# GpSimd's order around the half-tile norms, and evacuations ahead of sums in the last group

## The chip, the cores and the metric

The kernel runs on one core of a Trainium2 chip. The metric is the device time of one execution in microseconds (us). Five engines take part, each with its own queue that runs strictly in program order: TensorE (PE in the profile), VectorE (DVE), ScalarE (ACT), GpSimd (POOL) and SyncE (SP), which starts the DMAs. They wait for each other by semaphores.

## The reference

Three transformer-like blocks follow each other on a sequence of 1024 tokens of width 1024, all in float32.

```python
def reference(x, ...):
    x = first_block(x, ...)    # rmsnorm, conformer branch + HGRN2 branch, gates, w_out, rmsnorm
    x = second_block(x, ...)   # rmsnorm, attention / short conv / spatial gating, w_out, MLP, rmsnorm
    return third_block(x, ...) # mLSTM + pooling, w_out, layernorm, MLP, layernorm
```

What matters here are the places where a product's output is normed and goes into the next product:

```python
# end of the first block, start of the second
h_res = h_res + merged @ w_out                       # OUT1
x = rmsnorm(h_res[:, N_META:], final_g)
proj = rms_norm(x, mix_norm_g) @ w_in_2              # SGU, QKV, SHORT
# the second block's MLP
x = x + mixed @ w_out_2                              # OUT2
hdn = jnp.square(relu(rms_norm(x, mlp_norm_g) @ w_up))
x = x + hdn @ w_down                                 # MLP2
x = rms_norm(x, final_norm_g)
# the third block
u = x @ w_in_3                                       # GATES3 ...
x = layer_norm_3(ALPHA * x + y @ w_out_3, ...)       # OUT3
x = layer_norm_3(ALPHA * x + squared_relu_mlp(x, w_ff1, w_ff2), ...)   # MLP3
```

## The kernel before

**Layout.** Activations are kept transposed: 8 tiles `k` of 128 channels x 1024 tokens. A weight matrix is cut into 318 slabs of 128 x 1024; a slab makes one output tile of 128 channels from all 8 input tiles (or, in the MLP's way down, two tiles from four). Slab numbers start at `OUT1` = 88, `SGU` = 100, `OUT2` = 126, `MLP2` = 138, `GATES3` = 210, `OUT3` = 235, `MLP3` = 247.

**Products.** Each float32 operand is split into a high part (rounded to the matmul's format) and a low part (the rest). A product is three matmuls per input tile and 512 tokens: `hh` x `wh`, `hh` x `wl`, `hl` x `wh` (function `three`, L489, matmul at L505). So a slab needs

- `raw`, its weights by DMA, two buffers;
- `wh`, the rounded copy, by ScalarE (`split`, L1185), which waits until PE is through with the slab two before;
- `wl` = `raw` - `wh`, by GpSimd (`split`, L3114), two halves of 128 x 512, which PE waits for one by one; and
- for the first product after a norm, `hh` and `hl` of the tiles. ScalarE makes `hh` (`half_high`, L1494; `last_high`, L1928 to L1932, with the norm's offset). VectorE makes `hl` of tiles 0, 1, 2, 4 and 6, GpSimd that of tiles 3, 5 and 7 (`GP_TILES`; `half_low`, L3136).

**Half tiles.** Before each of four norms the last four output tiles are computed twice over, first for tokens 0 to 511 (half 0), then for 512 to 1023 (half 1): `gemm_half`. While PE computes half 1, the norm of half 0 is made. The stage behind the norm begins with four slabs for half 0, then the same four for half 1 (the weights are loaded and split again). The four places are OUT1 to `SGU` (norm `nx2`), OUT2 to `MLP2` (`ff2`), the end of MLP2 to `GATES3` (`nx3`), and OUT3 to `MLP3` (`ff3`).

**The norm itself.** VectorE evacuates a tile from PSUM, adding the residual (L2334, L2572, L2658, L2954). ScalarE squares it. VectorE adds the square to a sum over the tiles (L2345, L2583, L2893; for a layernorm the values too, L2885). When the last tile is added, PE multiplies the sums by ones to get a sum per token (L769, L934, L578 and L582), ScalarE and VectorE make the root and its inverse of it, and PE spreads these over the partitions (L588). VectorE multiplies the tiles with them (L2366, L2594, L2664, L2920 to L2923), reading the rows from PSUM. PE's part of the half-1 norm is a side job: it is issued between the products of the next stage's first slabs, the token sums after the fifth to seventh tile of the first one.

**What sets the order.** Each engine's program is written out by hand. `split(n)` makes all slabs up to `n` that are not made yet, so the place of a call sets how early a slab's parts stand in a queue. In `half_lows` GpSimd makes a slab's `wl` and the tiles' `hl` in turn; ScalarE's loops `for m, tiles in ...` do the same with `wh`, the squares and `hh`.

**The last group.** MLP3 ends with half tiles too, for tiles 2 to 7: PE writes each into one of two pairs of PSUM banks in turn (12 matmuls a tile), so a tile can start only when the tile two before is evacuated (`last_sums`, L3015). VectorE also subtracts an early mean from the tiles (`less_mean_2`, L3022), adds squares (`add_square`, L2893) and the values of the last tile (`last_value`, L2899), and norms the first half (`minus`, L3030, and `times`, L3036). PE's token sums for half 0 (`rest`, L578 and L582) are issued after the sixth tile step of half 1, that is two steps into its second product.

Of the kernel before, what the change touches and what calls it, by code (L numbers as in the profile page):

```python
# [57 lines left out]
SGU, QKV, SHORT, OUT2, MLP2 = 100, 108, 120, 126, 138  # L58
# [182 lines left out]
def program(nc, A, tables, draft):  # L241
# [929 lines left out]
    def scalar():  # L1171
# [4 lines left out]
        def split(n):  # L1176

            while done[0] <= min(n, NSLAB - 1):
                i = done[0]
                done[0] += 1  # L1180
                s = i % 2
                se.wait_ge(*c.weight_in[s](i))
                if i >= 2:
                    se.wait_ge(*spent(i - 2))
                se.activation(wh[:, s, :], raw[:, s, :], COPY).then_inc(*c.hi.tick(i))  # L1185
# [310 lines left out]
        def squares_out(m, *hf):  # L1496
            se.wait_ge(*c.ev_v("out", m, *hf))
            for n, (st, scale) in enumerate((("o1", 1.0), ("o2", V("final_g", m)))):
                dst, x = out_square(m, n), X[:, m, :]
                if m > 3:  # L1500
                    se.wait_ge(*(c.acc_v(st, 4, *hf) if m == 7 else c.acc_v(st, m - 3)))
                    dst, x = side_of(dst, *hf), side_of(x, *hf)
                se.activation(dst, x, SQUARE, scale=scale).then_inc(*c.sq.tick(st, m, *hf))
# [9 lines left out]
        def out_high(k, hf):  # L1513
            half_high("nx2", k, hf, half_slot(Cb[:, 4:8, :], k), c.nrm("nx2", k, hf))
# [11 lines left out]
        squares_out(7, 0)  # L1526
        split(OUT1 + 9)
        roots_out(0)
        for m, tiles in ((5, (0, 1)), (6, (2, 3, 4)), (7, (5, 6))):
            split(OUT1 + m + 5)  # L1530
            squares_out(m - 1, 1)
            for k in tiles:
                out_high(k, 0)
        squares_out(7, 1)
        split(SGU + 1)
        out_high(7, 0)
        roots_out(1)


# [150 lines left out]
        def half_mean_root(st, hf):  # L1690
            se.wait_ge(*c.tok(st, hf))
            se.activation(rr[:, 0, 4 * hf:4 * hf + 4], aux.of("tok", st, hf)[:, 0:4], SQRT, scale=1.0 / 1024,
                          bias=EPS).then_inc(*c.root.tick(st, hf))

        def mlp_high(k, hf):
            half_high("ff2", k, hf, half_slot(xn, k), c.nrm("ff2", k, hf))
# [42 lines left out]
        square("n5", 7, c.ev_v("x2", 7, 0), 0)  # L1739
        split(OUT2 + 9)  # L1740
        half_mean_root("n5", 0)
        for m, tiles in ((5, (0, 1)), (6, (2, 3, 4)), (7, (5, 6))):
            split(OUT2 + m + 5)
            square("n5", m - 1, c.ev_v("x2", m - 1, 1), 1)
            for k in tiles:
                mlp_high(k, 0)
        square("n5", 7, c.ev_v("x2", 7, 1), 1)
        split(MLP2 + 1)
        mlp_high(7, 0)
        half_mean_root("n5", 1)  # L1750
        first_ups(MLP2, t5, hdh, mlp_high)

# [18 lines left out]
        def in_high(k, hf):  # L1771
            half_high("nx3", k, hf, side_of(X[:, k, :], hf), c.nrm("fin2", k, hf))

        mlp(MLP2, t5, hdh)
        for hf, tiles in ((0, ((), (), (), ())), (1, ((), (0, 1), (2, 3, 4), (5, 6)))):
            i = down_at(MLP2, 7, 0, hf)
            split(i + 1)
            if hf:
                half_mean_root("n6", 0)
            for j in range(4):  # L1780
                if j:
                    split(i + j + 1)
                    square("n6", 2 * j - 1, c.ev_v("dn", MLP2, 7, 2 * j - 1, hf), hf)
                for k in tiles[j]:
                    in_high(k, 0)
                square("n6", 2 * j, c.ev_v("dn", MLP2, 7, 2 * j, hf), hf)
            square("n6", 7, c.ev_v("dn", MLP2, 7, 7, hf), hf)
        split(GATES3 + 1)
        in_high(7, 0)
        half_mean_root("n6", 1)  # L1790


# [163 lines left out]
        half_square("v1", 7, 0, c.ev_v("x3", 7, 0))  # L1956
        split(OUT3 + 9)
        half_root("v1", 0)
        todo = {5: (0, 1), 6: (2, 3, 4), 7: (5, 6)}
        for m in range(5, 8):  # L1960
            split(OUT3 + m + 5)
            half_square("v1", m - 1, 1, c.ev_v("x3", m - 1, 1))
            for k in todo[m]:
                last_high(k, 0)
        half_square("v1", 7, 1, c.ev_v("x3", 7, 1))
        split(MLP3 + 1)
        last_high(7, 0)
        half_root("v1", 1)

        first_ups(MLP3, t7, hdh3, last_high)  # L1970
# [46 lines left out]
    def vector():  # L2017
# [1037 lines left out]
            less_mean_2(k, 1)  # L3055
        last_sums(6, 0)
        add_square("v2", 3, 0)
        add_square("v2", 4, 0)
        for k in (5, 6, 7):
            less_mean_2(k, 1)  # L3060
        add_square("v2", 5, 0)
        last_sums(7, 0)
        last_value(0)
        add_square("v2", 6, 0)
        add_square("v2", 7, 0)
        half_stats("v2", 0)
        less_mean_2(0, 1)
        less_mean_2(1, 1)
        last_sums(2, 1)
        minus(0, 0)  # L3070
        minus(1, 0)
        add_square("v2", 1, 1)
        last_sums(3, 1)
        times(0, 0)
        times(1, 0)
        add_square("v2", 2, 1)
# [23 lines left out]
    def gpsimd():  # L3100
# [37 lines left out]
        def half_lows(ver, first, src):  # L3138

            for hf in range(2):  # L3140
                split(first + 4 * hf + 3)
                half_low(ver, 3, hf, src(3, hf))
                half_low(ver, 5, hf, src(5, hf))
                split(first + 4 * hf + 4)
                half_low(ver, 7, hf, src(7, hf))


        split(1)
# [492 lines left out]
```

## Time and profile before

| | us |
|---|---|
| runs shown, median (lowest to highest) | 3795.52 (3794.46 to 3797.2) |
| the profiled execution | 3796.67 |
| its span | 3795.4 |
| PE busy | 3690.3 |
| VectorE busy | 1720.7 |
| ScalarE busy | 1178.2 |
| GpSimd busy | 1091.7 |

All times in the rows below are from the span's start. "Busy" of PE covers overlapping matmuls, so it is not its peak. In a timeline a row is one instruction (or, with x2 and more, a run of like ones): start, duration, engine, line, operation, what it writes and reads. In square brackets stands the idle time before it that a semaphore ended, with the engine that released it. In a row of a stretch the busy time of each engine in it has the number of its instructions behind it, in brackets; the three numbers at the end are the mean granted clock of PE as a share of full speed, the DMA engines' share, and GB/s. `B` is the large buffer with the tiles (`X` in the code), `acc` and `t` are sums and squares.

### The profile page before, as it was taken

What the parts mean: (1) busy time and instruction counts of PE and PEld (TensorE: products, weight loads), DVE (VectorE), ACT (ScalarE), POOL (GpSimd) and SP (SyncE); (2) the same over time, 40 slices, a digit from 0 to 9 for tenths busy, and PEclk for the clock granted to TensorE, in tenths of its full rate; (3) what the DMA queues carried; (4) which work ended last, traced back from release to release, by engine and by line L of the source; (5) the groups of instructions that cost most, each with busy time, mean ns of one, the idle gap of its engine ahead of it and who ended that gap; (6) DMA issues with size and microseconds to landing.
All of it is one profiled execution on the core that took longest, in us unless ns stands there. A gap on an engine that the chain in (4) does not pass through costs nothing.

```text
span 3795.4 us, 42159 instructions
## 1 busy us (share of the span) xinstructions
PE 3690.3 (97%) x17644; PEld 3015.8 (79%) x17644; DVE 1720.7 (45%) x2132; ACT 1178.2 (31%) x1523; POOL 1091.7 (29%) x747
## 2 busy tenths in 40 slices
PE   6999999999999999999999999999999999999998
PEld 6989887888878876777788888887777788888886
DVE  5665615999543472225432222225667642222226
ACT  5555423222231344443321211114322331121113
POOL 3333321222233441112432222225113342222223
PEclk9999999999999999999999999999999999999999
DMA  2011021111232341101321111113101221111112
GB/s 102 28 30 33 23 78 50 56 56 56 72 137 96 103 132 35 37 27 36 106 67 50 45 48 48 46 49 126 44 28 51 89 72 45 51 45 47 48 46 76
DMA packets 64988, 229.29 MB, mean 60 GB/s; under 512 B 7200, under 2 KB 7328, under 8 KB 64672
## 3 DMA queue, kind: packets, MB, share of 16 engines
q1 hardware_dynamic: 64800, 226.60, 18.2%
q8 instruction: 140, 2.29, 0.2%
q14 instruction: 48, 0.39, 0.0%
HBM read 201.40 MB, written 25.17 MB: 60 GB/s over the span
## 4 chain that ended last, share of the span: by engine, by line
PE 88%; DVE 7%; ACT 2%; issue 1%; POOL 1%; DMA 1%; SPq 0%; DVEq 0%; ACTq 0%
PE psum L505 77%; PE psum L853 2%; PE psum L617 2%; PE psum L868 2%; PE psum L883 1%; DVE work L2171 1%; PE psum L588 1%; PE psum L739 0%; POOL wl L3114 0%; PE psum L702 0%; DVE qb L2173 0%; PE psum L641 0%; PE psum L640 0%; DVE fb L2094 0%; DVE k L2828 0%
## 5 line engine op out<-in xcount | busy, mean ns | idle before, releaser
L3114 POOL TENSOR_TENSOR wl<-raw,wh 128x512 fp32r<-128x512 f32 x636 | 882.7, 1408 | 2378.3 <-ACT wh L1185 2378.3
L505 PE MATMUL psum<-hh,wh 128*128 128x512 f32 (+2 forms) x3760 | 1186.8, 391 | 38.4 <-POOL wl L3114 15.7
L505 PE MATMUL psum<-hh,wl 128*128 128x512 f32 (+2 forms) x3760 | 1150.2, 382 | 0.0
L505 PE MATMUL psum<-hl,wh 128*128 128x512 f32 (+2 forms) x3760 | 1145.3, 380 | 0.0
L505 PEld LDWEIGHTS psum<-hh,wh 128*128 128x128 f32 x3760 | 676.2, 190 | 185.4 <-issue 30.9
L505 PEld LDWEIGHTS psum<-hh,wl 128*128 128x128 f32 x3760 | 699.4, 190 | 134.5
L505 PEld LDWEIGHTS psum<-hl,wh 128*128 128x128 f32 x3760 | 698.5, 190 | 133.2
L1185 ACT ACTIVATE wh<-raw 128x1024 fp32r<-128x1024 f32 x318 | 335.1, 1054 | 791.5 <-PE psum L505 785.0
L505 PE MATMUL psum<-hdh,wh 128*128 128x512 f32 x1024 | 333.9, 398 | 5.0 <-DVE B L3015 4.4
L505 PE MATMUL psum<-hdh,wl 128*128 128x512 f32 x1024 | 331.1, 395 | 0.0
L505 PE MATMUL psum<-hdl,wh 128*128 128x512 f32 x1024 | 331.1, 396 | 0.0
L2652 DVE TENSOR_TENSOR B<-B,psum 128x1024 f32<-128x1024 f32 x106 | 129.5, 1222 | 419.4 <-PE psum L505 419.4
L2632 DVE TENSOR_TENSOR t<-t 128x1024 f32<-128x1024 f32 (+1 forms) x72 | 90.5, 1257 | 471.1 <-ACT t L1764 471.1
L2222 DVE SCALAR_TENSOR_TENSOR psum<-av,vec,psum 128x1024 f32<-128x1024 f32 x232 | 299.2, 1290 | 7.8
L505 PEld LDWEIGHTS psum<-hdh,wh 128*128 128x128 f32 x1024 | 191.3, 188 | 57.7 <-DVE B L3015 6.1
L505 PEld LDWEIGHTS psum<-hdl,wh 128*128 128x128 f32 x1024 | 192.4, 188 | 46.4
L505 PEld LDWEIGHTS psum<-hdh,wl 128*128 128x128 f32 x1024 | 192.4, 188 | 45.9
L1764 ACT ACTIVATE t<-psum 128x1024 f32<-128x1024 f32 x56 | 57.4, 1024 | 426.2 <-PE psum L505 426.2
L3156 POOL TENSOR_TENSOR work<-fb 128x1024 f32<-128x1024 f32 x48 | 100.6, 2103 | 188.3 <-PE psum L617 140.1
L2493 DVE CUSTOM_DVE_ANT_0 pp<-psum,bias 128x640 f32<-128x640 f32 (+2 forms) x64 | 42.1, 658 | 194.4 <-PE psum L853 106.9
L2634 DVE TENSOR_TENSOR hdl<-t,hdh 128x1024 fp32r<-128x1024 f32 (+1 forms) x72 | 83.6, 1161 | 82.7 <-ACT hdh L1767 63.0
L1767 ACT ACTIVATE hdh<-t 128x1024 fp32r<-128x1024 f32 x56 | 59.3, 1059 | 72.3 <-DVE t L2632 72.3
(422 smaller groups left out, 3019.3 us busy)
## 6 DMA issues: line engine op xcount, KB each, us to landing
raw<-in_wts SPq DMA_DIRECT2D x318, 512.0 KB, 3.5
keep_x<-B SPq DMA_DIRECT2D x14, 512.0 KB, 5.8
X<-in_xin SPq DMA_DIRECT2D x8, 520.0 KB, 5.2
keep_sz<-tmp SPq DMA_DIRECT2D x8, 512.0 KB, 2.9
av<-keep_gr SPq DMA_DIRECT2D x8, 512.0 KB, 3.4
tmp<-keep_sz SPq DMA_DIRECT2D x8, 512.0 KB, 3.5
av<-keep_gc SPq DMA_DIRECT2D x8, 512.0 KB, 3.8
xc<-keep_x SPq DMA_DIRECT2D x8, 512.0 KB, 5.8
```

Of the source, the lines that this page charges most:

```text
L505: ins = pe.matmul(out, w, x[:, k, c0:c0 + width], start=first and n == 0, stop=final and n == 2)
L617: ins = pe.matmul(x[:, n * 128:(n + 1) * 128], left[:, cc], right[:, cc], start=True, stop=True)
L853: ins = pe.matmul(sp[:, a0:a0 + wd], qa[lo:lo + 64, s, i * 128:(i + 1) * 128], ka[lo:lo + 64, s, k0 + a0:k0 + a0 + wd], start=True, stop=True)
L868: ins = pe.matmul(OUT[:, 64 * i:64 * i + 64], pt_slot(j, m)[:, b_ * 128:(b_ + 1) * 128], va[:, s, a0:a0 + 64], start=(b_ == 0), stop=(b_ = ...
L1185: se.activation(wh[:, s, :], raw[:, s, :], COPY).then_inc(*c.hi.tick(i))
L1767: se.activation(xh[:, k, :], q, COPY).then_inc(*c.ml_act.tick("hi", base, u))
L2222: ve.scalar_tensor_tensor(Cb[:, m, :] if last else taps, u[:, j:j + T], V("conv_w", 8 * j + m), taps, MUL, ADD).then_inc(*c.cv_dve.tick(*( ...
L2632: ve.tensor_tensor(q, q, q, MUL).then_inc(*c.ml_dve.tick("sq", base, u, *hf))
L2634: ve.tensor_tensor(xl, q, fp(xh), SUB).then_inc(*c.ml_dve.tick("lo", base, u, *hf))
L2652: ve.tensor_tensor(X[:, m, :], X[:, m, :], flat(pairs.of(i, e)), ADD).then_inc(*c.ev_v.tick("dn", base, g, m))
L3114: gp.tensor_tensor(wl[:, s, a], raw[:, s, a], fp(wh[:, s, a]), SUB).then_inc(*c.lo.tick(i, p))
L3156: gp.tensor_tensor(lev(lv).rearrange("p (n b) -> p n b", b=2 * hs), bv, bv[:, :, hs - 1:hs].to_broadcast([P, T // (2 * hs), 2 * hs]), SUB) ...
```

## The change

It has three parts.

1. GpSimd (`half_lows`): at each of the eight places (four norms, two halves) the `wl` of the next half's first slab stands behind the low part of tile 3, ahead of those of 5 and 7. Before, it stood behind 5.
2. ScalarE: the high part of tile 7 (half 0) moves up to those of 5 and 6, and the `wh` of the stage's second slab goes ahead of the square of tile 7 (half 1).
3. VectorE, in the last group: the evacuation of tile 7 (half 0) stands ahead of the additions of squares 4 and 5, that of tile 2 (half 1) ahead of the addition of square 7 (half 0), that of tile 3 (half 1) one place forward.

```diff
@@ -1526,14 +1526,13 @@
         squares_out(7, 0)
         split(OUT1 + 9)
         roots_out(0)
-        for m, tiles in ((5, (0, 1)), (6, (2, 3, 4)), (7, (5, 6))):
+        for m, tiles in ((5, (0, 1)), (6, (2, 3, 4)), (7, (5, 6, 7))):
             split(OUT1 + m + 5)
             squares_out(m - 1, 1)
             for k in tiles:
                 out_high(k, 0)
+        split(SGU + 1)
         squares_out(7, 1)
-        split(SGU + 1)
-        out_high(7, 0)
         roots_out(1)
...
@@ -1772,11 +1770,12 @@
             half_high("nx3", k, hf, side_of(X[:, k, :], hf), c.nrm("fin2", k, hf))
 
         mlp(MLP2, t5, hdh)
-        for hf, tiles in ((0, ((), (), (), ())), (1, ((), (0, 1), (2, 3, 4), (5, 6)))):
+        for hf, tiles in ((0, ((), (), (), ())), (1, ((), (0, 1), (2, 3, 4), (5, 6, 7)))):
             i = down_at(MLP2, 7, 0, hf)
-            split(i + 1)
             if hf:
                 half_mean_root("n6", 0)
+            else:
+                split(i + 1)
             for j in range(4):
                 if j:
                     split(i + j + 1)
@@ -1784,9 +1783,8 @@
                 for k in tiles[j]:
                     in_high(k, 0)
                 square("n6", 2 * j, c.ev_v("dn", MLP2, 7, 2 * j, hf), hf)
+            split(i + 5)
             square("n6", 7, c.ev_v("dn", MLP2, 7, 7, hf), hf)
-        split(GATES3 + 1)
-        in_high(7, 0)
         half_mean_root("n6", 1)
@@ -1956,15 +1954,14 @@
         half_square("v1", 7, 0, c.ev_v("x3", 7, 0))
         split(OUT3 + 9)
         half_root("v1", 0)
-        todo = {5: (0, 1), 6: (2, 3, 4), 7: (5, 6)}
+        todo = {5: (0, 1), 6: (2, 3, 4), 7: (5, 6, 7)}
         for m in range(5, 8):
             split(OUT3 + m + 5)
             half_square("v1", m - 1, 1, c.ev_v("x3", m - 1, 1))
             for k in todo[m]:
                 last_high(k, 0)
+        split(MLP3 + 1)
         half_square("v1", 7, 1, c.ev_v("x3", 7, 1))
-        split(MLP3 + 1)
-        last_high(7, 0)
         half_root("v1", 1)
 
         first_ups(MLP3, t7, hdh3, last_high)
@@ -3055,22 +3052,22 @@
             less_mean_2(k, 1)
         last_sums(6, 0)
         add_square("v2", 3, 0)
+        last_sums(7, 0)
         add_square("v2", 4, 0)
         for k in (5, 6, 7):
             less_mean_2(k, 1)
         add_square("v2", 5, 0)
-        last_sums(7, 0)
         last_value(0)
         add_square("v2", 6, 0)
+        last_sums(2, 1)
         add_square("v2", 7, 0)
         half_stats("v2", 0)
         less_mean_2(0, 1)
         less_mean_2(1, 1)
-        last_sums(2, 1)
+        last_sums(3, 1)
         minus(0, 0)
         minus(1, 0)
         add_square("v2", 1, 1)
-        last_sums(3, 1)
         times(0, 0)
         times(1, 0)
         add_square("v2", 2, 1)
...
@@ -3138,11 +3135,9 @@
         def half_lows(ver, first, src):
 
             for hf in range(2):
-                split(first + 4 * hf + 3)
-                half_low(ver, 3, hf, src(3, hf))
-                half_low(ver, 5, hf, src(5, hf))
-                split(first + 4 * hf + 4)
-                half_low(ver, 7, hf, src(7, hf))
+                for n, k in enumerate(GP_TILES):
+                    split(first + 4 * hf + 3 + min(n, 1))
+                    half_low(ver, k, hf, src(k, hf))
 
 
         split(1)
```

The second hunk (norm `n5`, at `MLP2`), left out, is the first one's with other names. The instructions are the same in number and kind.

GpSimd, from the end of OUT3 (the run of 20 `wl` ends with the slab before `MLP3`'s first) into MLP3, before; `hl` are low parts of tiles, 3 and 5 in the first row of two, 7 in the next row:

```order
L3114 TENSOR_TENSOR wl<-raw,wh 128x512 x20
L3136 TENSOR_TENSOR hl<-B,hh 128x512 x2
L3114 TENSOR_TENSOR wl<-raw,wh 128x512 x2
L3136 TENSOR_TENSOR hl<-B,hh 128x512
L3114 TENSOR_TENSOR wl<-raw,wh 128x512 x6
L3136 TENSOR_TENSOR hl<-B,hh 128x512 x2
L3114 TENSOR_TENSOR wl<-raw,wh 128x512 x2
L3136 TENSOR_TENSOR hl<-B,hh 128x512
L3114 TENSOR_TENSOR wl<-raw,wh 128x512 x126
```

and now:

```order
L3111 TENSOR_TENSOR wl<-raw,wh 128x512 x20
L3133 TENSOR_TENSOR hl<-B,hh 128x512
L3111 TENSOR_TENSOR wl<-raw,wh 128x512 x2
L3133 TENSOR_TENSOR hl<-B,hh 128x512 x2
L3111 TENSOR_TENSOR wl<-raw,wh 128x512 x6
L3133 TENSOR_TENSOR hl<-B,hh 128x512
L3111 TENSOR_TENSOR wl<-raw,wh 128x512 x2
L3133 TENSOR_TENSOR hl<-B,hh 128x512 x2
L3111 TENSOR_TENSOR wl<-raw,wh 128x512 x126
```

The pair of `wl` is one slab. It changed places with the low part of tile 5, in both halves.

ScalarE, at the same place, from the `wh` of the first slab of `MLP3` on, before (L1916 is a square, L1928 with L1930 a high part of tile 5 or 7, L1932 that of another tile):

```order
L1185 ACTIVATE wh<-raw 128x1024
L1916 ACTIVATE t<-B 128x512
L1928 ACTIVATE B<-B,vec 128x512
L1930 ACTIVATE hh<-B 128x512
L1932 ACTIVATE hh<-B,vec 128x512
L1916 ACTIVATE t<-B 128x512
L1185 ACTIVATE wh<-raw 128x1024
L1928 ACTIVATE B<-B,vec 128x512
L1930 ACTIVATE hh<-B 128x512
L1921 ACTIVATE rr<-rr 128x4
```

and now (the same functions stand two lines higher):

```order
L1185 ACTIVATE wh<-raw 128x1024
L1914 ACTIVATE t<-B 128x512
L1926 ACTIVATE B<-B,vec 128x512
L1928 ACTIVATE hh<-B 128x512
L1930 ACTIVATE hh<-B,vec 128x512
L1926 ACTIVATE B<-B,vec 128x512
L1928 ACTIVATE hh<-B 128x512
L1185 ACTIVATE wh<-raw 128x1024
L1914 ACTIVATE t<-B 128x512
L1919 ACTIVATE rr<-rr 128x4
```

The high part of tile 7 and the `wh` of the second slab stand ahead of the last square.

VectorE in the last group, from the subtraction behind the evacuation of tile 6 of half 0 on, before (L3015 evacuates, L2893 adds a square, L2899 the values, L3022 subtracts the early mean, L2907 begins the norm's scalars):

```order
L3015 TENSOR_TENSOR B<-B,psum 128x512
L2893 TENSOR_TENSOR acc<-acc,t 128x512 x2
L3022 TENSOR_TENSOR B<-B,psum 128x512 x3
L2893 TENSOR_TENSOR acc<-acc,t 128x512
L3015 TENSOR_TENSOR B<-B,psum 128x512
L2899 TENSOR_TENSOR t<-t,B 128x512
L2893 TENSOR_TENSOR acc<-acc,t 128x512 x2
L2907 TENSOR_SCALAR rr<-psum 128x4
```

and now (three lines higher):

```order
L3012 TENSOR_TENSOR B<-B,psum 128x512
L2890 TENSOR_TENSOR acc<-acc,t 128x512
L3012 TENSOR_TENSOR B<-B,psum 128x512
L2890 TENSOR_TENSOR acc<-acc,t 128x512
L3019 TENSOR_TENSOR B<-B,psum 128x512 x3
L2890 TENSOR_TENSOR acc<-acc,t 128x512
L2896 TENSOR_TENSOR t<-t,B 128x512
L2890 TENSOR_TENSOR acc<-acc,t 128x512
L3012 TENSOR_TENSOR B<-B,psum 128x512
L2890 TENSOR_TENSOR acc<-acc,t 128x512
L2904 TENSOR_SCALAR rr<-psum 128x4
```

One evacuation moved up between the first two additions, and the next one, from below, in front of the last addition.

## Rows read from the trace of the kernel before

**Rows 1.** The page, section 1's first line: busy us, share of the span, instructions.
```profile
PE 3690.3 (97%) x17644; PEld 3015.8 (79%) x17644; DVE 1720.7 (45%) x2132; ACT 1178.2 (31%) x1523; POOL 1091.7 (29%) x747
```

**Rows 2.** Waits by releaser, whole execution: us in total, times, longest.
```profile
PE psum L505 <- POOL wl L3114: 15.7, 6, 5.1
...
PE psum L505 <- DVE B L3015: 4.4, 3, 2.8
```

**Rows 3.** Timeline of PE: start, duration, then the wait ended there and its releaser.
```profile
1351.71 0.47 PE L505 MATMUL psum<-hh,wh 128*128 128x512 f32 x1 [1.56 <-POOL wl L3114]
...
2609.26 0.47 PE L505 MATMUL psum<-hh,wh 128*128 128x512 f32 x1 [2.69 <-POOL wl L3114]
...
3036.59 0.68 PE L505 MATMUL psum<-hh,wh 128*128 128x512 f32 x1 [4.38 <-POOL wl L3114]
...
3064.76 0.47 PE L505 MATMUL psum<-hh,wh 128*128 128x512 f32 x1 [0.53 <-POOL wl L3114]
...
3751.35 0.50 PE L505 MATMUL psum<-hdh,wh 128*128 128x512 f32 x1 [2.76 <-DVE B L3015]
...
3757.56 0.50 PE L505 MATMUL psum<-hdh,wh 128*128 128x512 f32 x1 [1.37 <-DVE B L3015]
```

**Rows 4.** Stretches: length, busy us of PE, PEld, DVE, ACT, POOL; then granted clock.
```profile
1351.71:1356.65 4.94, 4.94 (x22) 4.03 (x23) 4.94 (x6) 2.08 (x3) 4.35 (x3) 1.00 0.39 108
2610.00:2613.40 3.40, 3.40 (x9) 2.63 (x8) 2.80 (x4) 1.86 (x3) 0.36 (x1) 0.50 0.48 154
3036.70:3040.10 3.40, 3.40 (x9) 2.63 (x10) 3.25 (x5) 2.44 (x4) 1.44 (x1) 0.50 0.15 42
3751.40:3757.50 6.10, 4.79 (x28) 3.91 (x28) 4.41 (x10) 1.93 (x5) 0.00 (x0) 1.00 0.00 0
```

**Rows 5.** Timelines of ACT, POOL, DVE and PE around the start of `MLP3`.
```profile
3029.96 1.05 ACT L1185 ACTIVATE wh<-raw 128x1024 fp32r<-128x1024 f32 x1
...
3022.33 2.99 POOL L3114 TENSOR_TENSOR wl<-raw,wh 128x512 fp32r<-128x512 f32 x2 [4.79 <-ACT wh L1185]
...
3035.18 2.96 POOL L3114 TENSOR_TENSOR wl<-raw,wh 128x512 fp32r<-128x512 f32 x2
...
3024.10 1.77 DVE L2893 TENSOR_TENSOR acc<-acc,t 128x512 f32<-128x512 f32 x1
...
3032.58 0.68 DVE L2893 TENSOR_TENSOR acc<-acc,t 128x512 f32<-128x512 f32 x1
...
3038.61 1.48 DVE L2893 TENSOR_TENSOR acc<-acc,t 128x512 f32<-128x512 f32 x2
...
3042.40 0.95 PE L578 MATMUL psum<-cst,t 128*128 128x1 f32 x8
```

**Rows 6.** Timelines of POOL, DVE and PE around the start of `GATES3`.
```profile
2607.39 2.96 POOL L3114 TENSOR_TENSOR wl<-raw,wh 128x512 fp32r<-128x512 f32 x2
...
2611.43 1.48 DVE L2583 TENSOR_TENSOR acc<-acc,t 128x512 f32<-128x512 f32 x2
...
2614.37 0.95 PE L934 MATMUL psum<-cst,acc 128*128 128x1 f32 x8
```

**Rows 7.** Timelines of DVE and PE around the start of `SGU`.
```profile
1347.23 0.68 DVE L2345 TENSOR_TENSOR Cb<-Cb,accc 128x512 f32<-128x512 f32 x1
...
1355.06 2.38 DVE L2345 TENSOR_TENSOR Cb<-Cb,tmp 128x512 f32<-128x512 f32 x2
...
1356.65 1.91 PE L769 MATMUL psum<-cst,Cb 128*128 128x1 f32 x16
```

**Rows 8.** Timelines of DVE and PE in the first slab of `MLP2`.
```profile
1886.17 1.74 DVE L2583 TENSOR_TENSOR acc<-acc,t 128x512 f32<-128x512 f32 x2
...
1889.03 0.95 PE L934 MATMUL psum<-cst,acc 128*128 128x1 f32 x8
```

**Rows 9.** Timeline of DVE in the last group.
```profile
3752.01 1.48 DVE L2893 TENSOR_TENSOR acc<-acc,t 128x512 f32<-128x512 f32 x2
...
3760.15 1.29 DVE L3030 TENSOR_TENSOR B<-B,psum 128x512 f32<-128x512 f32 x2 [2.65 <-PE psum L588]
```

More of the change, by code:

```diff
@@ L1741, in scalar @@
         half_mean_root("n5", 0)
-        for m, tiles in ((5, (0, 1)), (6, (2, 3, 4)), (7, (5, 6))):
+        for m, tiles in ((5, (0, 1)), (6, (2, 3, 4)), (7, (5, 6, 7))):
             split(OUT2 + m + 5)
@@ L1746, in scalar @@
                 mlp_high(k, 0)
+        split(MLP2 + 1)
         square("n5", 7, c.ev_v("x2", 7, 1), 1)
-        split(MLP2 + 1)
-        mlp_high(7, 0)
         half_mean_root("n5", 1)
```

## The prediction

> **What bounds the kernel now.** I read the page first: PE is busy 97% of the span [rows 1], so only what PE waits for can give time back. The waits by releaser come next. PE waits 15.7 us on GpSimd's `wl` in 6 waits and 4.4 us on VectorE's evacuations of the last group (L3015) in 3 [rows 2]. PE's timeline shows which of these the change touches [rows 3]:
>
> - the first slab of `SGU` starts at 1351.71 after a wait of 1.56 us on `wl`; that of `MLP2` has no wait;
> - the first slab of `GATES3` starts at 2609.26 after 2.69 us on `wl`;
> - the first slab of `MLP3` starts at 3036.59 after 4.38 us, and its fifth (the first of the second half) at 3064.76 after 0.53 us;
> - in the last group PE waits 2.76 us at 3751.35 and 1.37 us at 3757.56 on L3015.
>
> Together 13.3 us, 0.35% of the span: all that the change can aim at. Two of the starts are followed by 3.4 us at a granted clock of 0.50, the level of 1.2 GHz; 9 matmuls are counted there, 8 of them begun in it, one every 0.43 us, where of 22 in 4.94 us at full clock 21 were begun in it, one every 0.23 us [rows 4]. So such a stretch costs 8 x 0.20 = 1.6 us. The wait of 2.76 us in the last group, as long as the one at `GATES3`, was followed by full clock [rows 4].
>
> **Why the waits are there.** At each start GpSimd makes the low parts of tiles 3 and 5, then `wl` of the stage's first slab, then tile 7, while ScalarE makes `wh` of that slab before the high parts of 5 and 6. At `MLP3` `wh` ends at 3031.0, but GpSimd, held by tile 5, starts `wl` only at 3035.18, and PE starts 1.41 us after that [rows 3, 5].
>
> **The change part by part.** No instruction is added or removed and no DMA is moved. GpSimd now makes `wl` before the low parts of 5 and 7. At `MLP3` `wl` can start at 3031.1 and PE at 3032.5, 0.3 us after it is ready; tile 5 comes after `wl` (2.96 us for the pair) and half a pair's time, about 3035.6, and PE wants it after five tiles of 0.70 us, at 3036.0: little is lost there. I take all the start waits as gone.
>
> What is late next is the token sum. In the middle of the first slab PE multiplies the summed squares by ones (L769, L934, L578 with L582), and these need VectorE's last additions, which hang on the last evacuation of the stage before. That does not come earlier.
>
> At `MLP3` PE began the sums (of values first, then of squares some 0.8 us later) at 3042.40 [rows 5]. Without 4.38 us of wait and 1.6 of half clock it is there at 3036.4. VectorE's additions of squares end at 3038.61 + 1.48 = 3040.1, so the second set starts no earlier than that, against 3043.2: at best -3.1. Against it stands where GpSimd's work falls. Beside a pair of `wl` from 3022.33 an addition took 1.77 us (3024.10); with GpSimd idle the same addition of the next tile took 0.68 us (3032.58) [rows 5]. It and the one ahead of it now get the `wl` pair beside them: +2.1 us. The low part of 7 and the next `wl` come beside the last three additions: nothing to +2.5. In return what stood beside `wl` from 3035.2 to 3038.1 gets free. So between -3.1 and +1.5; I take -0.8, nearest to the pair of rows that measures it. The second half's start gains its 0.53.
>
> The rows show, then, that an addition of two SBUF tensors more than doubles beside GpSimd's work [rows 5]. The Trainium skill (GPSIMD Engine Reference, section 8, Key points) says that GpSimd shares its SBUF interfaces with VectorE and contends with instructions that read two SBUF inputs. By that rule the trace agrees. It speaks against this change, which puts GpSimd's work beside such additions; without it the term would be its best, -3.1.
>
> At `GATES3` the additions ended at 2611.43 + 1.48 = 2612.9. PE began the sums at 2614.37 and would be there at 2610.1 (2.69 and 1.6 less) [rows 6]. At best -1.45. GpSimd, which started `wl` at 2607.39, now has tile 7 and the next `wl` beside these two additions: up to +1.1 for each by the pair above, so +0.7 at worst. I take -0.6.
>
> At `SGU` the sums began at 1356.65 with no wait; PE would be there at 1355.1. The two additions of tile 7 took 2.38 us from 1355.06 [rows 7], with a `wl` beside them that is now over earlier; free, the first is done at 1355.7, at best -0.95. But the first `wl` moves on to the additions of tile 5, of which the one at 1347.23 took 0.68; at 1.19 each, as the later pair, this is +1.0, and VectorE has no gap from there on. Between -0.95 and +0.1; I take -0.3.
>
> At `MLP2` there is no start wait. The additions ended at 1886.17 + 1.74 = 1887.9 and the sums began at 1889.03 [rows 8]. The square of tile 7 now stands behind a `wh`, which takes 1.05 us [rows 5]; the last addition then ends at 1888.9 and the 1.1 us of slack covers it: 0, at worst +0.3. At the other three places the same 1.05 us is covered by VectorE, which is still at older work when the square is ready.
>
> In the last group tile 7's evacuation goes ahead of two additions of squares, that of tile 2 (second half) ahead of the last addition, that of 3 one place forward. PE no longer waits 2.76 us at 3751.35. But two tiles into that product it needs the sum of values (3752.0) and the last addition of squares, which ended at 3752.01 + 1.48 = 3753.5 [rows 9] and now has one more evacuation of 0.7 ahead: the sums end 0.7 later. The wait of 1.37 at 3757.56 goes, so PE's next product is 0.7 early, and so are VectorE's subtractions, which stood idle until PE's rows at 3760.15 [rows 9]. Behind them one evacuation less: another 0.7. From there VectorE works without a gap to the end of the group, so -1.4 stays. Bounds -2.0 (no new wait) and 0.
>
> Sum: -0.3 + 0 - 0.6 - 0.8 - 0.5 - 1.4 = -3.6 us.
>
> **The clock.** Waits at the starts turn into waits at the sums: 0.6 to 1.8 us at `SGU`, 2.8 to 4 at `GATES3`, 3.7 or more at `MLP3` and about 3 in the last group (both in two pieces, with 8 narrow matmuls between). The terms above took the half clock behind the old starts out; behind the new waits it would cost 1.6 each again. Of the old waits 4.38 and 2.69 were followed by it, 2.76 was not [rows 4]. I take it at 7 in 10 for `GATES3` and `MLP3` and 2 in 10 for the other two: 2.2 + 0.6 = +2.8.
>
> The Trainium skill (TensorE: Matmul & The Clock Gate, section HAM oscillation) says that a long wait between groups of matmuls makes the next group start at the lower clock. With that at all four places the sum would be +2.8, a rival below.
>
> So -3.6 + 2.8 = -0.8 us on the profiled execution's 3796.67 (span 3795.4 and 1.3 around it), 3795.9. The median of the runs shown is 1.15 lower, 3795.52, so 3794.7.
>
> **Rivals.**
> - The starts are kept: VectorE's additions are not held up and the clock stays full. -0.95 - 1.45 - 3.1 - 0.5 - 2.0 = -8.0, 3787.5. For it: PE is 97% busy and what goes was its wait. Against it: the additions grow beside GpSimd [rows 5].
> - Slower: half clock behind every new wait. Place: the products behind the token sums of `SGU`, `GATES3`, `MLP3` and the last group; price 4 x 1.6 = 6.4, so +2.8, 3798.3. It decides from waits of about 2.7 us on, where rows of both kinds exist; for it speaks that the narrow matmuls of the sums stand beside the wait and add little work.
> - Only the tail counts: at the starts the sums come no earlier than before, since `wl` beside the additions costs what it cost at 3024.10, and -1.4 remains: 3794.1.
>
> **How the numbers follow.** Forecast 0.50 (3791.5 to 3797), starts kept 0.15, half clock everywhere 0.25, tail only 0.10. The range, 3790.0 to 3798.5, leaves out most of the second case and the upper edge of the third. 0.2% is 7.6 us, about what a measurement of this kernel tells from no change: only the outer third of the second case is faster by that (0.05, with 0.01 for what I don't see), and slower by that needs the third case with every addition at its worst (0.03). The rest, 0.91, is within.
>
> **What would show it.** Right: at the starts GpSimd's `wl` stands directly behind `wh`, PE waits on VectorE's additions before L578, L934 and L769, and the additions of squares take longer on the mean. Wrong: PE reaches the second set of sums at `MLP3` more than 2 us earlier, or the clock stays 1.00 behind the new waits (faster than forecast); a wait on the low part of 5 or 7 inside a first slab; in the tail, VectorE's subtractions less than 0.3 us earlier.

## The result and the profile after

The changed kernel takes 3803.02 us in the median of 20 runs (3800.59 to 3805.91), the kernel before 3796.26 us beside it (20 runs, 3793.6 to 3798.48): a ratio of 1.0018, 95% interval 1.0011 to 1.0025. It is 6.8 us slower, and the range I gave (3790.0 to 3798.5) does not hold it.

The profiled execution took 3800.59 us, its span is 3799.3 us. From the page after, first line of section 1 (against [rows 1]):

```profile
PE 3690.3 (97%) x17644; PEld 3015.8 (79%) x17644; DVE 1728.1 (45%) x2132; ACT 1178.2 (31%) x1523; POOL 1095.7 (29%) x747
```

PE's work is the same. VectorE is busy 7.4 us longer with the same instructions and GpSimd 4.0 us; the rows below show that they slow each other down. The waits of PE by releaser (us in total, times, longest), against [rows 2]:

```profile
PE psum L505 <- POOL wl L3111: 6.9, 3, 5.0
...
PE psum L578 <- DVE t L2896: 4.9, 2, 3.4
...
PE psum L934 <- DVE acc L2580: 3.4, 2, 3.0
PE psum L582 <- DVE acc L2890: 3.2, 3, 2.2
...
PE psum L769 <- DVE Cb L2342: 2.6, 1, 2.6
PE psum L578 <- DVE t L2882: 2.6, 1, 2.6
...
PE psum L505 <- DVE B L3012: 0.3, 1, 0.3
```

The waits on `wl` went from 15.7 us to 6.9 (5.0 of it is a wait that the change doesn't touch), those on the last group's evacuations from 4.4 to 0.3. In their place stand waits at the token sums: L769 (`SGU`), L934 (mostly `GATES3`), L578 and L582 (`MLP3`, and the last group as L2896; of its 4.9 us, 3.4 are the very last wait, which was 3.1 before). Of the start waits two leave a rest: 1.00 us at `GATES3`, where PE now waits for VectorE's evacuation (L2655), and 0.42 us on `wl` at `MLP3`. PE's timeline at these places, against [rows 3, 5 to 8]:

```profile
1354.43 1.92 PE L769 MATMUL psum<-cst,Cb 128*128 128x1 f32 x16 [2.62 <-DVE Cb L2342]
...
2607.28 0.51 PE L505 MATMUL psum<-hh,wh 128*128 128x512 f32 x1 [1.00 <-DVE B L2655]
...
2614.01 1.02 PE L934 MATMUL psum<-cst,acc 128*128 128x1 f32 x8 [2.96 <-DVE acc L2580]
...
3034.95 0.47 PE L505 MATMUL psum<-hh,wh 128*128 128x512 f32 x1 [0.42 <-POOL wl L3111]
...
3041.95 1.07 PE L578 MATMUL psum<-cst,t 128*128 128x1 f32 x8 [2.59 <-DVE t L2882]
3045.21 1.86 PE L582 MATMUL psum<-cst,acc 128*128 128x1 f32 x8 [2.19 <-DVE acc L2890]
...
3756.33 1.02 PE L578 MATMUL psum<-cst,t 128*128 128x1 f32 x8 [1.49 <-DVE t L2896]
3758.03 1.05 PE L582 MATMUL psum<-cst,acc 128*128 128x1 f32 x8 [0.69 <-DVE acc L2890]
```

And the clock behind them, in stretches with the columns of [rows 4]:

```profile
1356.60:1360.00 3.40, 3.40 (x10) 2.62 (x9) 3.00 (x9) 0.63 (x2) 0.00 (x0) 0.50 1.01 389
2616.10:2619.50 3.40, 3.40 (x13) 3.03 (x13) 0.97 (x2) 0.00 (x0) 0.00 (x0) 0.50 0.38 146
3042.80:3053.00 10.20, 8.01 (x26) 6.77 (x26) 2.92 (x6) 1.75 (x3) 4.98 (x5) 0.50 0.16 51
3759.60:3763.00 3.40, 3.40 (x10) 2.63 (x9) 2.12 (x5) 2.46 (x5) 0.01 (x1) 0.50 0.02 5
```

Half clock (a granted clock of 0.50, the level of 1.2 GHz) stands behind the new waits at all four places. Before there was none behind the sums of `SGU` and of the last group's half 0; at `GATES3` it was 3.4 us, as now, and at `MLP3` 3.4 us where it is 10.2 now. For `SGU` the stretch of the kernel before, against the first one above:

```profile
1358.60:1362.00 3.40, 3.40 (x16) 2.75 (x16) 3.21 (x8) 0.25 (x2) 0.00 (x0) 1.00 0.56 131
```

PE's large matmuls (L505) stand in the same order in both programs, so the n-th of one can be set against the n-th of the other, both counted from the first matmul. The difference in time between the two (plus: the changed kernel is behind) is called the shift here. Read just ahead of and behind each place, it says what the place cost:

| place | difference ahead | behind | cost us |
|---|---|---|---|
| `SGU` | -3.1 | -0.6 | +2.5 |
| `MLP2` | -0.6 | -0.2 | +0.5 |
| `GATES3` | -0.2 | +1.5 | +1.6 |
| `MLP3`, both halves | +2.5 | +5.0 | +2.5 |
| last group, to the last large matmul | +5.0 | +4.5 | -0.5 |
| from there to the end | +4.5 | +4.0 | -0.5 |

The places sum to +6.1 us; the medians say +6.8. The spans of the profiled pair differ by only 3.9: this execution was 3.1 us ahead before the first place, and 1.0 behind between `GATES3` and `MLP3`, where nothing was changed. Stretches of half clock stand there too, and not always at the same instructions. In the first 600 us the profile of before has 17.0 us of them and that of the changed kernel 3.4. Between `GATES3` and `MLP3` the lag grows inside two stretches that both have (10.2 us from 2668.0 and 6.8 us from 2934.3 before). Differences of under 3 us between two single profiles are therefore read place by place here, not from the spans.

### The profile page after: what moved, and what is told of

Read it like the earlier page. It is cut to its first block, busy times and chain, and to the rows that moved or that the text cites. A ratio compares the mean times of both kernels' runs of the same rounds, so it can differ in the third digit from the quotient of the medians.

```text
span 3799.3 us, 42159 instructions
## 1 busy us (share of the span) xinstructions
PE 3690.3 (97%) x17644; PEld 3015.8 (79%) x17644; DVE 1728.1 (45%) x2132; ACT 1178.2 (31%) x1523; POOL 1095.7 (29%) x747
## 4 chain that ended last, share of the span: by engine, by line
PE 88%; DVE 8%; issue 2%; ACT 1%; DMA 1%; POOL 0%; SPq 0%; DVEq 0%; ACTq 0%
PE psum L505 76%; PE psum L853 2%; PE psum L617 2%; PE psum L868 2%; PE psum L883 1%; DVE work L2168 1%; PE psum L588 1%; DVE acc L2890 0%; PE psum L739 0%; DVE qb L2170 0%; PE psum L702 0%; PE psum L641 0%; PE psum L640 0%; DVE fb L2091 0%; DVE fb L2083 0%
## 5 line engine op out<-in xcount | busy, mean ns | idle before, releaser
L505 PE MATMUL psum<-hh,wh 128*128 128x512 f32 (+2 forms) x3760 | 1185.2, 391 | 31.0 <-POOL wl L3111 6.9
L505 PE MATMUL psum<-hh,wl 128*128 128x512 f32 (+2 forms) x3760 | 1149.2, 381 | 0.0
L505 PE MATMUL psum<-hl,wh 128*128 128x512 f32 (+2 forms) x3760 | 1144.9, 380 | 0.0
L505 PEld LDWEIGHTS psum<-hh,wh 128*128 128x128 f32 x3760 | 675.4, 190 | 175.9 <-issue 20.7
L505 PEld LDWEIGHTS psum<-hh,wl 128*128 128x128 f32 x3760 | 698.3, 189 | 134.7
L505 PEld LDWEIGHTS psum<-hl,wh 128*128 128x128 f32 x3760 | 697.4, 189 | 133.0
L505 PE MATMUL psum<-hdh,wh 128*128 128x512 f32 x1024 | 334.6, 399 | 0.9 <-DVE hdl L2631 0.5
L505 PE MATMUL psum<-hdl,wh 128*128 128x512 f32 x1024 | 331.8, 396 | 0.0
L505 PE MATMUL psum<-hdh,wl 128*128 128x512 f32 x1024 | 331.7, 396 | 0.0
L505 PEld LDWEIGHTS psum<-hdh,wh 128*128 128x128 f32 x1024 | 191.6, 188 | 53.0 <-DVE B L2649 4.9
L505 PEld LDWEIGHTS psum<-hdl,wh 128*128 128x128 f32 x1024 | 192.8, 188 | 46.6
L505 PEld LDWEIGHTS psum<-hdh,wl 128*128 128x128 f32 x1024 | 192.9, 188 | 46.2
```

Source lines behind the costliest of these rows:

```text
L505: ins = pe.matmul(out, w, x[:, k, c0:c0 + width], start=first and n == 0, stop=final and n == 2)
```

## The experiments

Each was timed beside the kernel before on the same chip, in 11 runs; the kernel before had 27 or 33. A ratio is to the kernel before, with its 95% interval, which is about 0.1% (3.5 us) to either side. "Shift" is meant as above, between a kernel's profile and that of before. Where a median is set against the changed kernel's 3803.02, the two are from different sets; set each against the kernel before beside it, and such a difference changes by at most 0.8 us.

### Each part alone

The first kernel has only the new `half_lows` of the diff, the second only the four changes on ScalarE, the third only the new order of `last_sums` and `add_square`.

> The kernel before with GpSimd's new order alone (wl ahead of the low parts of tiles 5 and 7, at all eight places). Contention theory: the whole loss comes from this part, because it puts wl and the low part of 7 beside VectorE's last additions, so PE's wait moves to the token sums and the clock halves behind it: 5 to 8 us slower than before, with waits before L578, L934 and L769 of 2 us and more. ScalarE theory (the last square now stands behind a wh and is what the additions wait for): GpSimd's order alone then gives time back, 2 to 5 us faster than before.

> The kernel before with ScalarE's moves alone (high part of tile 7 and wh of the second slab ahead of the last square). Contention theory: within 1.5 us of before; the start waits on wl stay 15 to 16 us in sum, and the last addition of squares is no more than 0.5 us later. ScalarE theory: this part alone is 3 us or more slower, with the wait at the sums of squares (L582, L934) longer by about the 1.05 us of a wh at each place.

> The kernel before with VectorE's new order in the last group alone. My prediction's term: 1.4 us faster than before, with PE's waits on the evacuations of the last group going from 4.4 us to under 1. Rival (the wait only moves to the sums L578/L582, and half clock comes behind it): between 0.5 us faster and 1 us slower.

| kernel | median | beside | ratio |
|---|---|---|---|
| GpSimd alone | 3799.13 | 3796.46 | 1.0005 (0.9996 to 1.0014) |
| ScalarE alone | 3798.19 | 3796.46 | 1.0006 (0.9997 to 1.0015) |
| last group alone | 3795.95 | 3796.46 | 0.9998 (0.9989 to 1.0007) |

Neither theory of the first two was right in size: +2.7, +1.7 and -0.5 us (none of them settled by its interval) make 3.9 where the whole has 6.8. The profiles say why. VectorE and GpSimd at `MLP3`, GpSimd's order alone:

```profile
3033.98 3.11 POOL L3114 TENSOR_TENSOR wl<-raw,wh 128x512 fp32r<-128x512 f32 x2 [1.02 <-ACT wh L1185]
...
3044.62 1.26 POOL L3136 TENSOR_TENSOR hl<-B,hh 128x512 fp32r<-128x512 f32 x1 [5.83 <-ACT hh L1930]
...
3035.86 1.78 DVE L2893 TENSOR_TENSOR acc<-acc,t 128x512 f32<-128x512 f32 x1
...
3042.31 1.48 DVE L2893 TENSOR_TENSOR acc<-acc,t 128x512 f32<-128x512 f32 x2
```

and the whole change:

```profile
3033.41 3.10 POOL L3111 TENSOR_TENSOR wl<-raw,wh 128x512 fp32r<-128x512 f32 x2 [1.04 <-ACT wh L1185]
...
3041.31 1.62 POOL L3133 TENSOR_TENSOR hl<-B,hh 128x512 fp32r<-128x512 f32 x1 [3.10 <-ACT hh L1928]
3042.89 3.38 POOL L3111 TENSOR_TENSOR wl<-raw,wh 128x512 fp32r<-128x512 f32 x2
...
3035.28 1.78 DVE L2890 TENSOR_TENSOR acc<-acc,t 128x512 f32<-128x512 f32 x1
...
3041.72 3.44 DVE L2890 TENSOR_TENSOR acc<-acc,t 128x512 f32<-128x512 f32 x2
```

In both, the `wl` that moved ahead lies beside the addition that took 0.68 us at 3032.58 in [rows 5] and makes it 1.78. But the last two additions take 1.48 us when GpSimd is idle and 3.44 when ScalarE's early high part of tile 7 lets GpSimd make its low part and the next `wl` at once. At `GATES3` it is the same: 1.48 us in [rows 6], 2.99 in the changed kernel. With ScalarE's part alone the last pair is just as slow (3.46 and 2.87 us), but the shifts across the two places (`GATES3`, `MLP3`) are only +0.2 and 0.0: PE, still held at the start by `wl`, comes to the sums late enough. With GpSimd's part alone they are +0.1 and -0.2: there PE gains at the start and loses about as much at the sums, by waits of 1.45 and 2.56 us and the half clock behind them (3.4 and 6.8 us). One part slows the last additions, the other takes away the slack that hid it, so the two cost more together. At `SGU` each part alone costs: the shift across it is +2.9 us with GpSimd's order (6.8 us at half clock behind the sums) and +2.5 with ScalarE's (3.4 us). ScalarE's alone, VectorE's last pair there (2.38 us in [rows 7]) and the stretch behind the sums:

```profile
1354.66 3.39 DVE L2342 TENSOR_TENSOR Cb<-Cb,tmp 128x512 f32<-128x512 f32 x2
```

```profile
1359.90:1363.30 3.40, 3.40 (x10) 2.62 (x9) 2.86 (x9) 0.76 (x2) 0.00 (x0) 0.50 1.02 359
```

The kernel before had full clock there. The wait at the second set of sums is only 0.56 us.

The last group alone: PE's waits on its evacuations are gone, as the term said, and PE is 3.0 us ahead at the product that waited 2.76 us. Then come waits of 1.5 and 0.7 us at the sums and 6.8 us of half clock from 3753.9 on, and the shift across the group ends at +0.5. The rival's account holds.

### The high part of tile 7 back

```diff
-            for m, tiles in ((5, (0, 1)), (6, (2, 3, 4)), (7, (5, 6, 7))):
+            for m, tiles in ((5, (0, 1)), (6, (2, 3, 4)), (7, (5, 6))):
...
         split(SGU + 1)
         squares_out(7, 1)
+        out_high(7, 0)
```

and the same at the other three places.

> The changed kernel with the high part of tile 7 (half 0) back behind the last square on ScalarE at SGU, MLP2, GATES3 and MLP3; all else as in it. Theory: it is the early high part of 7 that lets GpSimd put its low part and the next wl beside VectorE's last two additions (2.99 us at GATES3, 3.44 at MLP3 where they were 1.48). With it back they take 1.5 to 1.8 us again, the waits before L934 and L582 shrink by 1.5 and 2.0 us, and the kernel is 2.5 to 4 us faster than the changed one: 3799 to 3800.5. Rival (the additions at tile 5 and 6, slowed by the first wl, are what counts): within 1 us of the changed kernel.

3797.76 us beside 3797.02, ratio 1.0001 (0.9992 to 1.0010): 5.3 us below the changed kernel's 3803.02 (6.0 when each is set against the kernel before beside it), more than expected. VectorE at `MLP3`:

```profile
3035.92 1.78 DVE L2894 TENSOR_TENSOR acc<-acc,t 128x512 f32<-128x512 f32 x1
...
3042.37 1.48 DVE L2894 TENSOR_TENSOR acc<-acc,t 128x512 f32<-128x512 f32 x2
```

The slow middle addition stays, the last pair is back at 1.48 us (at `GATES3` too), and the shifts across the two places are +0.1 and -0.3 us instead of +1.6 and +2.5. The early high part of tile 7 is what turned an even trade into a loss there. That holds although half clock still stands behind the sums, 3.4 us at `GATES3` and 6.8 at `MLP3`. `SGU` still costs +3.2, with 6.8 us at half clock.

### Token sums three tiles later

```diff
-            yield from pause(6)
+            yield from pause(6 if hf == 0 else 9)
             x = grab(aux, ("tok", "o", hf), c.inv("o2", hf, "mean"))
```

and so for `rest_square` (4 to 7) and `rest` (5 to 8), half 1 only.

> The changed kernel with PE's token sums of the second half three tiles (2.1 us) later in the first slab of SGU, MLP2, GATES3 and MLP3, the rows behind them as far behind the sums as before. If the additions being late is what costs (contention theory), the waits of 2.6, 3.0 and 4.8 us at the sums shrink by 2.1 us each and little or no half clock is left there: 6 to 12 us faster than the changed kernel, 3791 to 3797. Rival (the chain from the sums to the second half's normed tiles has no slack): the time comes back as waits in front of the fifth slab of these stages, and the kernel is no faster than the changed one, 3802 or more.

3796.56 us beside 3796.46, ratio 0.9999 (0.9991 to 1.0008): 6.5 us below the changed kernel, as the first theory had it, but level with the kernel before, though the start waits are gone. At `MLP3` PE met other waits:

```profile
3031.38 0.47 PE L505 MATMUL psum<-hh,wh 128*128 128x512 f32 x1 [0.41 <-POOL wl L3111]
...
3036.96 0.50 PE L505 MATMUL psum<-hh,wh 128*128 128x512 f32 x1 [1.17 <-DVE hl L2927]
...
3039.41 0.79 PE L505 MATMUL psum<-hh,wh 128*128 128x512 f32 x1 [1.49 <-POOL hl L3133]
```

```profile
3038.90:3049.10 10.20, 9.56 (x30) 7.82 (x31) 3.25 (x6) 1.86 (x4) 4.57 (x4) 0.50 0.17 51
2615.70:2619.10 3.40, 3.40 (x13) 3.00 (x13) 1.33 (x2) 1.47 (x2) 2.40 (x2) 0.51 0.33 135
```

The tiles themselves are not ready for a PE that starts 4 us early: 6 and 7 come late. And the half clock is there again behind these waits, at `GATES3` behind one of only 0.95 us. So at `MLP3` the later sums gave nothing: the shift across it is +2.5 as in the changed kernel. They gave at `SGU` (+0.6 for +2.5), `MLP2` (-0.2 for +0.5) and `GATES3` (-0.4 for +1.6).

### Dummy matmuls in the waits

What does the half clock cost, and do the waits bring it? A function that keeps PE at work while it would wait:

```diff
+        def fill(n, dst):
+            for _ in range(n):
+                pe.matmul(dst, hh[:, 0, META:META + 128], hh[:, 0, META:META + 496], start=True, stop=True)
...
+            fill(first, x[:, 16:512])
             pe.wait_ge(*c.acc_v(st, "sum", hf))
```

It writes part of a PSUM bank that is free at the time; nothing reads it.

> The changed kernel with dummy matmuls (128x128 by 496 columns, results overwritten) ahead of the waits for the token sums: 10 at SGU, 12 at GATES3, 10 and 8 at MLP3, about as long as PE waits there. They take PE no time it has use for. If the waits bring the half clock behind them, SGU, GATES3 and MLP3 run at full clock and 1.6 + 1.6 + 4.8 = 8 us go: 3794 to 3797. Rival (the half clock comes from something else, the waits only stand near it): within 1.5 us of the changed kernel, or slower by what the dummies outlast the waits.

> The kernel before with dummy matmuls of the same kind inside the start waits: 11 at GATES3 (2.7 us waited), 18 at MLP3 (4.4 us). If the waits bring the half clock behind them, both stretches of 3.4 us at half clock go and the kernel is 3 us faster than before, 3793 to 3794. Rival: as before, within 1 us.

> The changed kernel with token sums three tiles later, and with dummy matmuls in the waits that this left: 1 at SGU and 3 at GATES3 ahead of the sums, 4 and 5 ahead of tiles 6 and 7 in the first slab of MLP3. If what the later sums alone did not give back is half clock behind these waits (10.2 us of it at MLP3, 3.4 at SGU and GATES3 each, 8 us in all), this is 5 to 8 us faster than the later sums alone: 3789 to 3792. Rival (the tiles themselves and what comes behind hold PE, the clock only follows): 3795 or more.

| kernel | median | beside | ratio |
|---|---|---|---|
| changed, with dummies | 3797.73 | 3797.02 | 1.0002 (0.9993 to 1.0010) |
| before, with dummies | 3797.43 | 3797.02 | 0.9998 (0.9989 to 1.0007) |
| changed, later sums, dummies | 3793.98 | 3797.02 | 0.9990 (0.9981 to 0.9999) |

The changed kernel gets 5.3 us faster by 40 matmuls more; 8 us had been expected. The stretches behind the sums of `GATES3`, `MLP3` and `SGU` in it:

```profile
2616.10:2619.50 3.40, 3.40 (x23) 3.04 (x24) 0.48 (x2) 0.17 (x1) 0.68 (x1) 1.00 0.44 136
3040.80:3051.00 10.20, 9.71 (x58) 8.31 (x59) 5.56 (x10) 2.80 (x6) 7.04 (x5) 1.00 0.16 53
1358.60:1362.00 3.40, 3.40 (x10) 2.65 (x9) 2.74 (x9) 0.88 (x2) 0.00 (x0) 0.50 0.96 374
```

Full clock (1.00, the level of 2.4 GHz) at the first two, at the third not. The shift across `GATES3` is 0.0 and across `MLP3` -1.1 us, where the changed kernel had +1.6 and +2.5: so the half clock behind the new waits cost 1.6 and 3.6 us. At `SGU` the shift is still +2.4.

With the kernel before I was wrong, and the profile shows how. Both starts run at full clock now, and PE is 3.4 us ahead when the last group begins (2.8 of it from the two places, where 3 had been expected in all). Then, behind the same wait of 2.76 us that was followed by full clock in [rows 4]:

```profile
3747.66 0.50 PE L505 MATMUL psum<-hdh,wh 128*128 128x512 f32 x1 [2.76 <-DVE B L3021]
```

```profile
3034.40:3037.80 3.40, 3.40 (x15) 2.77 (x16) 3.26 (x5) 2.26 (x4) 1.63 (x1) 1.00 0.18 28
3748.10:3758.30 10.20, 10.10 (x33) 8.13 (x32) 4.03 (x10) 3.17 (x6) 0.89 (x1) 0.50 0.01 2
```

10.2 us at half clock, which take the gain back (shift 0.0 behind the group). A wait of this length may or may not be followed by half clock; none followed in the profiles of the kernel before, of GpSimd's part alone and of ScalarE's part alone. That a wait is spared it in one profile says little.

The third kernel is faster than the kernel before, if barely, and 2.6 us below the later sums alone, where 5 to 8 had been expected: with the sums later and the waits filled, the half clock at `GATES3` and `MLP3` is gone, and the shift stands at -2.9 behind the last group.

### All waits filled

The last three fill the last group's waits as well (5 and 2 dummies ahead of the sums of half 0, 13 ahead of those of half 1, 2 ahead of the rows). The second sets `SGU` back. The third has the order of before at all four norms, with 11 dummies in the start wait of `GATES3` and 18 in that of `MLP3`; its start wait at `SGU` (1.55 us, with full clock behind it) is left as it is.

> The changed kernel with sums three tiles later and dummy matmuls in all the waits left: those of the last run of this kind (GATES3 3, MLP3 4 and 5), 2 and 1 ahead of the two sets of sums at SGU, and in the last group 5 and 2 ahead of the sums of half 0 (waits of 1.5 and 0.7 us), 13 ahead of those of half 1 (3.4 us) and 2 ahead of the rows. If half clock behind waits is what is left, SGU (3.4 us of it) gives 1.6, the middle of the last group 1.6, and its end 1 us more: 3 to 4 us faster than the later sums with dummies at GATES3 and MLP3 alone, so 3789.5 to 3791. Rival (half clock turns up at the next pause instead, as in the last group of the kernel before with dummies at the starts): no gain over 3794.

> The run before it in this set, with SGU set back: GpSimd's and ScalarE's order and the place of the token sums there as in the kernel before, no dummies there. Theory: at SGU VectorE is busy from the evacuations to the sums, so the new order gains 1.7 us at the start and loses all of it in slowed additions; as in the kernel before there is no half clock there. Within 1 us of the run before it, or up to 1.5 us faster if SGU keeps its half clock there. Rival (the start's 1.56 us are a gain that stays, with the clock kept): 1.5 us slower than it.

> The kernel before with VectorE's new order in the last group and dummy matmuls in the start waits (11 at GATES3, 18 at MLP3) and in the last group (5, 2, 13 and 2, as above). If the order of GpSimd and ScalarE gives nothing of its own and all there is to have is the clock: 3789.5 to 3792, level with the first run of this set. Rival (the starts, once they are not paid for, are worth 2 us and more at GATES3 and MLP3): 2 to 4 us slower than the first run of this set.

| kernel | median | beside | ratio |
|---|---|---|---|
| changed, later sums, all filled | 3790.23 | 3796.18 | 0.9984 (0.9975 to 0.9993) |
| the same, `SGU` as before | 3791.57 | 3796.18 | 0.9988 (0.9979 to 0.9997) |
| before, last group's order new, all filled | 3790.29 | 3796.18 | 0.9984 (0.9975 to 0.9993) |

The last group in the first of them:

```profile
3747.90:3758.10 10.20, 10.01 (x59) 8.50 (x60) 7.70 (x16) 3.42 (x6) 3.47 (x3) 1.00 0.01 2
```

and in the last:

```profile
3749.60:3759.80 10.20, 10.01 (x59) 8.52 (x60) 7.71 (x16) 3.43 (x6) 3.48 (x3) 1.00 0.00 0
```

Both are 6 us faster than the kernel before and 12.8 faster than the changed one (medians of different sets). They differ by 0.06 us, so the order that GpSimd and ScalarE got in this change, with the sums later, gives nothing that these medians can tell. Place by place the first has `GATES3` at -2.1 and `MLP3` at -1.7 us against -1.2 and -1.6 in the third, but +0.6 against 0.0 at `SGU`, where its dummies did not keep the clock. The last group's order is worth 1.9 us (the shift across it in both).

Setting `SGU` back gave no gain: +1.3 us, within the interval. Its profile has full clock at `SGU` and a shift of 0.0 across it, where the run before it has +0.6 with 3.4 us at half clock. But it had 3.4 us of half clock in `MLP3` from 3044.9 on, in instructions that are the same in both. This experiment is inconclusive on time; on the clock it says that at `SGU` the half clock came with the new order, in spite of dummies, and went with the old one, which had none.

## Why the prediction was wrong

Its terms against what was measured. "Order" is the shift across a place with the half clock behind the new waits taken out: at `GATES3` and `MLP3` that of the changed kernel with dummies, in the last group that of the first kernel of the last set; at `SGU`, where dummies did not help, the changed kernel's less 1.6 us for its 3.4 us at half clock, an estimate by the price of such a stretch in [rows 4]; no run shows the clock's cost at `SGU` by itself. "Clock" is what is left.

| place | order, predicted | measured | clock, predicted | measured |
|---|---|---|---|---|
| `SGU` | -0.3 | +0.9 | +0.3 | +1.6 |
| `MLP2` | 0 | +0.5 | 0 | 0 |
| `GATES3` | -0.6 | 0.0 | +1.1 | +1.6 |
| `MLP3` | -1.3 | -1.1 | +1.1 | +3.6 |
| last group | -1.4 | -1.9 | +0.3 | +1.4 |
| end | | -0.5 | | |
| sum | -3.6 | -2.1 | +2.8 | +8.2 |

The clock's term is the step that failed: 5.4 of the 6.9 us between -0.8 and +6.1; for the 0.7 us more in the medians no cause is shown. I took the half clock at 7 in 10 for `GATES3` and `MLP3` and 2 in 10 for the other two, with a price of 1.6 us each; it came behind all four, and at `MLP3`, with two waits in a row, it lasted 10.2 us and cost 3.6. The other 1.5 us are the order, which gave 2.1 us where I had 3.6; most of that is `SGU`. My rival "half clock behind every new wait" had its place right and its price wrong: 6.4 us where 8.2 was measured; its 3798.3 is still 4.7 us below the median.

- **The start waits go, and PE waits at the sums.** Right but for the 1.00 us that `GATES3` kept (I took all the start waits as gone), at the lines named, with 2.6 us at `SGU` (0.6 to 1.8 said), 3.0 at `GATES3` (2.8 to 4 said), 4.8 at `MLP3` (3.7 or more said), 2.2 in the last group (about 3 said).
- **Additions slow down beside GpSimd.** Right: 0.68 to 1.78 us at `MLP3`, and VectorE's busy time is up 7.4 us. The last three there, which I gave "nothing to +2.5", took 1.6 more (0.69 and 3.44 us for 1.06 and 1.48); the two that I gave +2.1 took 1.5 more (1.06 and 1.78 for 0.69 and 0.68). The Trainium skill (GPSIMD Engine Reference, section 8, Key points) names instructions with two SBUF inputs as those that contend with GpSimd. The trace agrees: the additions grew, and the subtraction L2917, which reads PSUM, took 0.67 us at 3036.98 beside GpSimd's low part. What I had not seen is that ScalarE's part decides whether the last pair is slowed.
- **`SGU`.** My upper bound, +0.1, was too low. I bounded the loss at the additions of tile 5 by 1.0. They took 1.63 and 1.78 us instead of 0.68 each (the first two rows below), 2.05 more. The two additions of squares behind them took 3.05 us, and 2.86 before (last row): a `wl` stood beside them in both kernels, now that of the second slab. The last pair gave back 1.10 us, with 1.28 for 2.38, as I had it. VectorE has no gap there to hide any of it.

```profile
1343.41 1.63 DVE L2342 TENSOR_TENSOR Cb<-Cb,tmp 128x512 f32<-128x512 f32 x1
1344.97 1.78 DVE L2342 TENSOR_TENSOR Cb<-Cb,accc 128x512 f32<-128x512 f32 x1
...
1349.32 3.05 DVE L2342 TENSOR_TENSOR Cb<-Cb,sg 128x512 f32<-128x512 f32 x2
...
1353.61 1.28 DVE L2342 TENSOR_TENSOR Cb<-Cb,tmp 128x512 f32<-128x512 f32 x2
```

and in the kernel before:

```profile
1350.96 2.86 DVE L2345 TENSOR_TENSOR Cb<-Cb,sg 128x512 f32<-128x512 f32 x2
```

- **`MLP2`.** The additions took 3.10 us instead of 1.74 [rows 8], since GpSimd's low part of tile 7 and its next `wl` fell beside them. I had only counted the 1.05 us of the square's delay. PE waited 0.42 us.
- **`GATES3` and `MLP3`, order.** 0.6 and 0.2 us off, within their bounds.
- **The best case.** "The starts are kept", 3787.5, was reached by no kernel: with the sums out of the way PE waited on the low parts of tiles 6 and 7 at `MLP3`. Of the 4.0 us that its start had gained, 2.7 went there. `wl` was only the last of several things that come at about the same time.
- **The last group.** Right in kind, and -1.9 with the clock kept. With it not kept, 1.4 of it was lost in the changed kernel.

That dummies in the waits raise the clock and give the time back is shown at `GATES3`, `MLP3` and in the last group, each on two kernels. At `SGU` they did not, and what brings the half clock there stays open: the sums are 16 narrow matmuls, and in the eight profiles with a new order there (of either engine) a stretch of half clock stood behind them, after waits of 0.2 to 2.6 us and once after none; in the five with the old order none did. The Trainium skill (TensorE: Matmul & The Clock Gate, section HAM oscillation) tells of the lower clock behind long waits; the rows here have it behind short ones too, down to 0.95 us at `GATES3` (with later sums, and a wait of 1.00 us at the start of the slab).

## What to carry to other kernels

A wait removed from a nearly full engine is worth its length only if nothing that engine needs next is late; list every input of the next few microseconds, not just the first (here token sums, then tiles 6 and 7). Where the clock can halve behind a wait, price a moved wait with that, take the worst for two waits in a row, and try to fill the waits with work of no use. Fill all of them: 29 dummies at two starts gave nothing in the median, since the half clock came behind the next wait, and 37 or 51 there and in the last group gave 6 us, 1.9 of them by the last group's order. And before putting GpSimd's work earlier, look at what VectorE does at that time: here additions of two SBUF tensors took up to 1.78 us for 0.68 beside it.

## What the runs showed of the hardware

- The same wait of 2.76 us in the last group was followed by full clock in the kernel before and by 10.2 us at half clock in the same kernel with dummies, the last of them over 700 us ahead of it.
- An addition of two SBUF tensors (128x512) took 0.68 to 0.69 us alone and up to 1.78 beside a `wl` (changed kernel, 3035.28); the subtraction that reads PSUM kept its 0.67 to 0.68 us. GpSimd's low part took 1.26 to 1.30 us alone (3044.62 with GpSimd's order alone) and 1.62 to 1.75 beside VectorE's additions.
- In the changed kernel 12 dummy matmuls in the wait at `GATES3` and 18 in the two at `MLP3` brought the clock behind them from 0.50 to 1.00.
